# One program per engine for the router and expert stages, with the gather's operands and the last residual reordered

## What is computed

```python
h = rms_norm(x, p["norm2_g"]) * (1.0 + sc2) + sh2
x = x + g2 * moe(h, ...)          # 64 experts, 6 per token, and a shared expert
y = rms_norm(x, final_norm_g)

# moe: top 6 of 64 experts per token, then
a = einsum("td,edf->tef", x, w1)
b = einsum("td,edf->tef", x, w3)
act = silu(a) * b * gates
routed = einsum("tef,efd->td", act, w2)
shared = (silu(x @ ws1) * (x @ ws3)) @ ws2
```

## Time and profile before

| | us |
|---|---|
| three timed runs | 1001.08, 1001.49, 1003.55 (median 1001.49) |
| the profiled execution, whole | 1000.73 |
| its span, first to last instruction | 998.9 |
| PE busy / DVE busy / ACT busy in it | 898.0 / 411.2 / 194.8 |
| DMA over the span | 272.52 MB, mean 273 GB/s |

### The profile page before, as it was taken

How to read it: one execution, slowest core, us unless ns; L and a number is a source line. 1 busy time by engine, 2 the same in 40 slices (tenths; PEclk the granted TensorE clock), 3 DMA queues, 4 the chain that set the end, 5 groups by cost and what they waited for, 6 DMA issues and landing times.

```text
span 998.9 us, 14344 instructions
## 1 busy us (share of the span) xinstructions
PE 898.0 (90%) x5664; PEld 489.4 (49%) x5664; DVE 411.2 (41%) x1006; ACT 194.8 (20%) x422; POOL 99.9 (10%) x100
## 2 busy tenths in 40 slices
PE   2879998999998999979799999899899899899873
PEld 2545767655675554436535345245245245345332
DVE  4695495797021133255323343233223223223137
ACT  4123325100213000150311111211211211211212
POOL 0499970000000000000000000000000000000000
PEclk9678999999997999979899999999999999999996
DMA  9995136120408503012987999999999999999971
GB/s 257 345 368 228 44 127 212 43 85 0 185 20 323 211 1 126 1 63 80 426 345 311 423 425 427 425 426 427 426 426 424 414 425 426 427 425 401 379 320 63
DMA packets 50088, 272.52 MB, mean 273 GB/s; under 512 B 5729, under 2 KB 14343, under 8 KB 21535
## 3 DMA queue, kind: packets, MB, share of 16 engines
q1 hardware_dynamic: 48706, 267.31, 66.1%
q10 hardware_dynamic: 1312, 4.25, 1.4%
HBM read 268.30 MB, written 3.24 MB: 272 GB/s over the span
## 4 chain that ended last, share of the span: by engine, by line
PE 35%; DMA 9%; DVE 3%; SPq 2%; issue 1%; ACT 1%; DVEq 0%
PE bank L1752 15%; PE bank L1789 7%; PE bank L1728 7%; PE bank L1773 5%; DMA sb<-w 4%; DMA sb_W<-w 3%; DMA sb_W<-x_dram 2%; SPq L1129 1%; DVE sb L1911 1%; SPq L1135 0%; ACT sb_Y L1841 0%; DVE sb_W L1978 0%; DVE sb L1977 0%; DVE sb_H L2095 0%; ACT sb L1836 0%
## 5 line engine op out<-in xcount | busy, mean ns | idle before, releaser
L1752 PE MATMUL bank<-sb 128*32 128x512 f32 (+2 forms) x1312 | 188.5, 604 | 12.5 <-DMA sb<-w 6.5
L1752 PEld LDWEIGHTS bank<-sb 128*32 128x32 f32 (+2 forms) x1312 | 56.1, 115 | 110.9 <-issue 110.0
L1728 PE MATMUL bank<-sb_Y,sb_ST 128*128 128x512 f32 x312 | 84.9, 423 | 11.5 <-DVE sb_Y L2013 9.1
L1773 PE MATMUL bank<-sb 128*32 128x512 f32 (+2 forms) x552 | 87.4, 596 | 4.7 <-ACT sb L1836 4.7
L750 PE MATMUL bank<-early 128*128 128x384 f32 x256 | 82.8, 486 | 0.0
L1789 PE MATMUL bank<-sb_S,sb_H 128*128 128x512 f32 (+1 forms) x336 | 75.8, 386 | 6.9 <-ACT sb_H L1868 4.0
L1911 DVE TENSOR_TENSOR sb<-sb,bank 128x512 f32<-128x512 f32 x78 | 53.7, 688 | 62.4 <-PE bank L1728 61.2
L1728 PEld LDWEIGHTS bank<-sb_Y,sb_ST 128*128 128x128 f32 x312 | 56.2, 196 | 45.9 <-issue 20.9
L1789 PEld LDWEIGHTS bank<-sb_S,sb_H 128*128 128x128 f32 x336 | 60.8, 195 | 24.6 <-issue 5.5
L1752 PE MATMUL bank<-sb_W,sb 128*32 128x512 f32 (+1 forms) x160 | 61.2, 635 | 4.9 <-DMA sb<-w 4.9
L750 PEld LDWEIGHTS bank<-early 128*128 128x128 f32 x256 | 48.6, 190 | 33.9 <-issue 0.2
(11 more groups left out here) (289 smaller groups left out, 1104.1 us busy)
## 6 DMA issues: line engine op xcount, KB each, us to landing
sb<-w SPq DMA_DIRECT2D x161, 1024.0 KB, 17.1
sb_W<-w SPq DMA_DIRECT2D x31, 1024.0 KB, 19.5
sb<-w_ada SPq DMA_DIRECT2D x15, 1024.0 KB, 9.1
early<-w_in SPq DMA_DIRECT2D x12, 1024.0 KB, 7.9
early<-w_ada SPq DMA_DIRECT2D x9, 1024.0 KB, 25.5
sb<-w_out SPq DMA_DIRECT2D x1, 4096.0 KB, 17.2
sb<-ada_dram SPq DMA_DIRECT2D x6, 512.0 KB, 15.5
early<-w_proj_s SPq DMA_DIRECT2D x1, 2560.0 KB, 15.4
```

Of the source, the lines that this page charges most:

```text
L1728: ins = nc.tensor.matmul(bank[m % 2][:, :], ST[:, p, j * P:(j + 1) * P], YR[:, x, p % 2, 512 * h:512 * h + 512], start=p == ps[0] and x == ...
L1752: ins = nc.tensor.matmul(bank[2 + p % 2][c0:c0 + w, :], XT[:, c, P * p + c0:P * p + c0 + w], gate_up_weights(units)[:, :, c, :], start=c = ...
L1773: ins = nc.tensor.matmul(bank[y_bank[p][h]][c0:c0 + w, :], hidT[:, f, c0:c0 + w], down_weights(units)[:, f, 512 * h:512 * h + 512], start= ...
```

## The change

The third and fourth block become one block, so that the engines no longer meet between them. Each engine's program of the fourth block follows directly on that of the third. In detail:

- ACT makes Hh between the two SiLUs of the shared expert instead of at the start of the fourth block. DVE fills the gate matrix and makes Hl after cap_full (L1501), ahead of its wait for the positions (PB_DONE), and `block_slots(0)` right after posB and GB.
- New waits: SP waits for the first S (S_ok) and for all products of the shared expert (sy_mm 6) before it loads final_norm_g and the rest of the weights. PE waits for pos_ok ahead of chunk 1 of the first gather and for all eight copies of sy_ok (the shared expert's six and two of the positions) ahead of the first `hidden`. DVE waits for those eight copies ahead of batch 0.
- Memory: sb_W, sb_Y, sb_S, sb_ST, sb_g, sb_fin and sb_H get other places; the residual of the third block (XR), w_s2 and tmpE move too.
- g2b is loaded with a count of its own (g2_in) after `gate_up(6, 3)` and ahead of the last six down weights. The load of X stays behind all weights and waits for units 12 and 13 only.
- DVE in the last batch: ACC times g2b for j = 0 after `add`, for j = 1 and 2 after `down(2)`; X plus ACC for all three after `down(3)`.

```diff
+                sp.wait_ge(S_ok, 1)
+                sp.wait_ge(sy_mm, 2 * NT)
...
                     gate_up(b, 3)
+                    if b == NB - 1:
+                        kind, r = LAST_USER[N_UNITS - 1]
+                        sp.wait_ge(dict(h=h_mm, d=y1_mm)[kind], r + 1)
+                        for r in range(2):
+                            sp.dma_start(g2b[:, r, :], ada_dram[r, 5 * D:6 * D].partition_broadcast(P)).then_inc(g2_in, 16)
                     downward(b, 2)
                     downward(b, 3)
...
-                for u in range(UNITS_SB, N_UNITS):
+                for u in (UNITS_SB, UNITS_SB + 1):
                     kind, r = LAST_USER[u]
                     sp.wait_ge(dict(h=h_mm, d=y1_mm)[kind], r + 1)
-                for r in range(2):
-                    sp.dma_start(g2b[:, r, :], ada_dram[r, 5 * D:6 * D].partition_broadcast(P)).then_inc(fin_in, 16)
                 sp.dma_start(X, x2_dram).then_inc(fin_in, 16)
...
                         if c == 1:
                             wait_last(pe, y_low, rd(2))
+                            if B.first:
+                                pe.wait_ge(pos_ok, 1)
...
                     pe.wait_ge(gates_ok, bt(1, 1))
+                    if B.first:
+                        pe.wait_ge(sy_ok, 2 * NT + 2)
                     hidden(0)
...
                     nc.scalar.activation(hs[:, f], bank[2 + 2 * f][:, 0:TOK], ACT.Silu).then_inc(sh_si, 1)
+                    if f == 0:
+                        act.wait_ge(H_ok, 3)
+                        for j in range(NT):
+                            nc.scalar.activation(Hh[:, j], H[:, j], ACT.Copy).then_inc(h_high_ok, 1)
...
                 ts(cap_full, const[0:E, C_ONE:C_ONE + P], cap_c, float(SB), ALU.mult, ALU.mult).then_inc(sel_ok, 1)
+                ts(k64, iota[:, 0:BATCH], float(SL), float(SL), ALU.mult, ALU.add).then_inc(acc_ok, 1)
+                for x in range(2):
+                    step(ts(gates_id[:, :, x, 0:GC], ...))
+                    nc.vector.tensor_copy(gates_id[:, :, x, GC:GW], ...)
+                for j in range(NT):
+                    dve.wait_ge(h_high_ok, j + 1)
+                    tt(Hl[:, j], H[:, j], Hh[:, j].bitcast(F32), ALU.subtract).then_inc(h_low_ok, 1)
                 dve.wait_ge(pos_mm, PB_DONE)
...
+                block_slots(0)
                 dve.wait_ge(pos_mm, CAP_DONE)
...
-                def before_residual(j):
+                def gated(j):
 
                     if j == 0:
-                        dve.wait_ge(fin_in, 64)
-                    step(tt(ACC[:, j], ACC[:, j], g2b[:, min(j, 1)], ALU.mult))
+                        dve.wait_ge(g2_in, 32)
+                        dve.wait_ge(acc_ok, 12 * NB - 5)
+                    tt(ACC[:, j], ACC[:, j], g2b[:, min(j, 1)], ALU.mult).then_inc(gated_ok, 1)
+
+                def to_residual(j):
+
+                    if j == 0:
+                        dve.wait_ge(fin_in, 32)
+                    dve.wait_ge(gated_ok, j + 1)
                     step(tt(X[:, j], X[:, j], ACC[:, j], ALU.add))
...
                         add(bt, 0)
                         if B.last:
-                            before_residual(0)
+                            gated(0)
                         down(2)
                         if B.last:
-                            before_residual(1)
+                            gated(1)
+                            gated(2)
                         down(3)
                         if B.last:
-                            before_residual(2)
+                            for j in range(NT):
+                                to_residual(j)
...
+                dve.wait_ge(sy_ok, 2 * NT + 2)
                 n = batches(dve, body, overflow_first, overflow_last).per_batch
```

More of the change, by code:

```diff
@@ new lines, in build, with wait_last, __init__, per_batch @@
+        g2_in, gated_ok = sem("g2_in"), sem("gated_ok")
+        NB = len(PLAN)
+        rounds_before = [sum(len(r) for r in ROUNDS[:b]) for b in range(NB)]
+        assert all(len(r) == 4 for r in ROUNDS[1:]) and len(ROUNDS[0]) == 2
+        y_bank = [(5, 6), (5, 6), (5, 6), (2, 1)]
+        def wait_last(eng, s, value):
+            if not isinstance(value, int) or value > 0:
+                eng.wait_ge(s, value)
+        class Static:
+            def __init__(self, b):
+                self.b, self.rounds, self.first, self.last, self.tail = b, ROUNDS[b], b == 0, b == NB - 1, False
+                self.slots = P * len(self.rounds)
+            def per_batch(self, per, off=0):
+                return self.b * per + off
+            def per_round(self, per, off=0):
+                return rounds_before[self.b] * per + off
+            def experts(self, p):
+                return [(c0, w) for c0, w, _ in self.rounds[p]]
+            def weights(self, kind, p):
+                out = []
+                for c0, w, place in self.rounds[p]:
+                    units, _, loaded = UNIT_OF[kind, place]
+                    out.append((c0, w, units, [in_first_stages[u] + n for u, n in zip(units, loaded)]))
+                return out
@@ new lines, in column_tiles, with batches @@
+        def column_tiles(experts):
+            wide = min(w if w != 96 else SB for _, w, *_ in experts)
+            return [(c, wide, *rest) for c0, w, *rest in experts for c in range(c0, c0 + w, wide)]
+        def batches(eng, body, first=None, after=None):
+            for b in range(NB):
+                body(Static(b))
+            eng.wait_ge(tail_ok, 1)
+            more = eng.value_load(ids[0:1, 0:1], min_val=0, max_val=MAXT // BATCH)
+            with eng.If(more > 0):
+                if first:
+                    first()
+                with eng.Fori(0, more) as b:
+                    body(Tail4(b))
+                if after:
+                    after(Tail4(more).tail_batch)
+            return Tail4(more)
@@ L1316, in _ @@
+                scatter(batches(pe, body), -6, 0, (2, 3))
             @block.scalar
@@ L1332, in _ @@
                         act.wait_ge(n2_sq, j)
-                    nc.scalar.activation(at(o_U, D), X[:, j], ACT.Square,
+                    nc.scalar.activation(at(o_U, D), XR[:, j], ACT.Square,
                                          accum_out=nst[:, j:j + 1]).then_inc(n2_sq, 1)
```

623 lines of the change are left out of this document (283 added, 340 removed).

## The result

| | before | after | ratio, 95% interval |
|---|---|---|---|
| first comparison, six runs each | 1001.95 (1000.17 to 1003.55) | 992.0 (988.57 to 992.83) | 0.9892 [0.9872, 0.9913] |
| the same kernel again, later: nine and five runs | 1001.24 (999.62 to 1002.16) | 988.39 (985.11 to 990.02) | 0.9866 [0.9846, 0.9886] |

All times in us. The change makes the kernel faster by 10 to 13 us; the eleven runs of after have their median at 988.9. The forecast was 987.0 with a range of 985.0 to 991.0: the first median lies 1.0 above that range, the second inside it. A second profile of after comes from the later comparison (988.49 us, span 986.7).

The account below looks back on a forecast made before the run. Expert weight loads set the pace from about 550 to 900 us, so PE's first hidden product and DVE's work after X count: 998.9 - 7.9 - 6.1 = 984.9, plus 1.83 is 986.7, forecast 987.0, range 985.0 to 991.0.

Parts of the forecast that it names:

- The front: Shared expert's last product to first hidden product: with the work moved ahead, the hidden product starts 7.9 us sooner.
- the other end (5.8): First gather on PE: if it takes 8.1 us instead of 5.9, the first hidden product gains only 5.8 us.
- The cover on ACT and DVE: Waits in the shared expert: 2.95 us of Hh fit ACT's 12.43, 4.8 us of work fit DVE's 6.42, 1.6 spare.
- That it is carried to the end: Expert weight stream: later loads wait for products, so the dense stretch starts the full 7.9 us sooner, near 541.
- the rival of the slower moved tiles: Loads into moved units 12 to 14: from 0.45 us more per load, over 31 loads, the kernel is slower; 3%.
- The end: After X lands: g2b's products move into DVE's wait, three additions remain, and the residual comes 6.1 us sooner.
- the one on the six down weights: Loads behind g2b: they land 2.5 us later; down(3) delayed by none or 1.4 us, none taken, else gain 4.7.
- the prediction's own sign: At down(3): the forecast is wrong if down(3) waits for a transfer for more than 1.4 us.
- the two counts of 962.4 and 964.1: Last down weight's landing before the change: 962.4 counted forward from the last hidden weights, 964.1 counted back from X.
- The stream swallows the front: Loads between 505 and 549 bound by bytes, not releases: only the end gains, 994.6 us; 6%.
- The end gives nothing: g2b ahead of the six loads holds down(3) back until DVE is as late as before: 992.8 us; 7%.
- It doesn't do what it says: Hl overruns its cover on DVE, PE still stands before the gather, the end is lost: about 1001 us; 3%.

Follow-up runs that it names:

- e5_work_behind: Changed kernel, still one block, with Hh, the gate matrix fill, block_slots(0) and Hl put back behind the shared expert; 996.25 us, ratio 0.9965.
- e9_sums_between: Changed kernel with g2b issued before the last pair of gate and up loads, and DVE's sums with X placed among down(3)'s low parts; 987.87 us.
- e2_end_only: Kernel before with only the new order of g2b's load, the products with it and the sums with X; 996.98 us, ratio 0.9971.
- e8_products_before_down: Changed kernel with 16 transposes of the identity on PE ahead of down(3)'s wait for weights; 989.96 us, ratio 0.9882.
- e3_gates_behind: Changed kernel with g2b's load moved back behind the six down weights, DVE's new order kept; 988.21 us, ratio 0.988.
- e10_products_before_hidden: e9_sums_between plus 20 transposes ahead of the last hidden product's wait for weights, its hid_ok wait moved ahead of both; 985.12 us, ratio 0.9847.

## Why the prediction was right or wrong

**The front: right in size, place and cause.** 7.99 us against 7.9. Gather at a clock of 1.00, as forecast, so the other end (5.8) didn't come. The cover on ACT and DVE held, with 2.10 us left where 1.6 was worked out. In e5_work_behind the same work put behind the shared expert takes all of it back. The rule that the forecast weighed here (the Trainium skill, "TensorE: Matmul & The Clock Gate", "What's actually happening": activity releases the throttle, idling brings it back) agrees: 1.00 without a stand, 0.76 in the stretch with two stands.

**That it is carried to the end: right.** The dense stretch starts at 541 us in the second execution of after, as forecast, and near 545 in the first, which was 2.8 us late already ahead of the gather. 2.3 us of DMA idle are left where 1.2 was forecast. The stretch to the last hidden product but one grew by 0.7 and 1.0 us against the first profile of before. Over all executions with the moved tiles it lies between 438.9 (e5_work_behind) and 442.7 (e9_sums_between), with the old places between 440.5 and 440.8. That speaks against the rival of the slower moved tiles: even 2 us over 31 loads are 0.06 each, and 0.45 was its threshold.

**The end: the mechanism right, one term of the sum mis-sized.** The step that failed is the one on the six down weights: "I take none, being nearer to the row that PE itself shows; the other end is a gain of 4.7." The end gained 4.8 us in the second execution of after and 4.9 in e2_end_only: it was the other end. Also by the prediction's own sign the step was wrong, since `down(3)` waited for a transfer for 2.40 and 1.92 us, more than 1.4. Two sizes were off, and that the other end came out so closely is in part luck. The first is when the last weight landed before: at 963.3, between the two counts of 962.4 and 964.1, so 1.9 us ahead of `down(3)`. The second is the price of g2b ahead of the weights. The sum took 2.5 us, 1 MiB at the rate of the dense stretch; the last weight landed some 3.3 us later (26.6 to 27.0 us behind the last hidden product but one, against 23.4 to 23.6). The trace of before had this price too: there g2b landed at 966.5, 3.1 us behind the last weight. So the count back from X, which also took g2b at 2.5, was 0.8 too late, the delay was 0.8 too short, and their sum, 26.7, was right. The row of PE that I leaned on, `down(3)` waiting for ACT alone, said only that the weight had landed by then, not how long before.

A term that the sum didn't have at all: behind the stand of 2.40 us that this wait makes `down(3)` takes 5.11 us in the first execution, at a mean granted clock of 0.71. That is 1.5 us more, and the end there gained 3.0. I priced the wait and not what PE's clock may do behind it, though the front's argument had just been made of that. Why the clock was low there and not behind the stands of 1.92 and 1.97 us in the second execution and in e2_end_only stays open; one execution shows it.

The first execution against the forecast of its span, 984.9, term by term from the table (the second in brackets): stages ahead of the change +3.2 (+0.3), to the shared product -0.4 (-0.3), the front -0.1 (-0.1), the rounds +0.7 (+1.0), the end +3.1 (+1.3), behind it -0.4 (-0.3). Together +6.1 (+1.8), which are 991.0 and 986.7. The forecast of 987.0 had moreover taken only part of the offset of the median: 986.7 and 0.76 are 987.5.

**The range: the scatter was mis-sized.** I gave the runs' own scatter as 0.4 us. The runs shown spread by 2.5, those of the second table line by 4.9, fourteen runs of before from 998.51 to 1003.98. The term of +3.2 is a piece of it: nothing that the change touches runs there. Windows of 10 us out of that stretch, first after, then after's second execution, then before:

```profile
163.00:173.00 10.00, 9.16 (x84) 7.32 (x84) 0.75 (x2) 3.96 (x12) 0.00 (x0) 0.52 0.91 288
```

```profile
163.00:173.00 10.00, 9.31 (x137) 7.47 (x138) 0.51 (x2) 5.94 (x18) 0.00 (x0) 0.83 0.84 266
```

```profile
163.00:173.00 10.00, 9.58 (x139) 7.85 (x140) 0.25 (x2) 6.13 (x20) 0.00 (x0) 0.83 0.86 273
```

The same code, behind a stand of 2.79, 3.19 and 2.72 us: 84 products in one execution and 137 or 139 in the others, at a granted clock of 0.52 and 0.83. The twelve other profiled executions of this work reach L750 at 178.2 to 180.4 us. With a scatter of 4 us in the range the first median would have lain in it. Whether the other high runs of the first comparison (992.0 to 992.5) were high for the same reason isn't known: only one of the six has a profile. The second median, 988.39, lies below the 988.9 that the range's upper end makes without its 2.1 for a slow gather, which didn't come; the first lies above all of it.

**The rivals.** The stream swallows the front: no (990.38 with the front alone). The end gives nothing: no, but its mechanism, g2b ahead of the six weights, is the one that took 1.3 of the 6.1 us, and 3.1 with the low clock behind the wait. It doesn't do what it says: no. Slower by the moved tiles: no.

Open: whether the order with the sums between is faster on the clock than the change. Its trace is, by 3.7 us behind the last hidden product against the second execution of after, but with g2b in the gap that product starts 8.5 to 10.3 us behind the one before it (four executions), where it was 7.6 to 7.9; that gives 0.6 us or more of it back, and 987.87 against 988.39 can't be told apart with these runs.

## What to carry to other kernels

A load that is pulled forward for one engine stands in front of others on the same queue: find when the last of those lands in the trace of before, and price the load by what that same load took there (3.1 us for g2b) and not by the rate of the dense stretch (2.5). A wait that ends on something else says nothing of how much slack there was. Price a new stand of PE twice, once for the wait and once, as the range's other end, for the product behind it at the lower clock. And where a kernel's PE stands often, its single executions differ by more than their medians suggest: look at the spread of the runs that are there before setting the ends of a range.

## What the runs showed of the hardware that was not expected

How long PE stood, here between 2.8 and 3.7 us, doesn't tell at which clock it goes on. The last hidden product, 64 products of one shape, takes 7.07 us behind its wait for weights, or 8.3 to 8.8. Its waits and durations in different executions: 2.77 us and 7.07 (after), 2.89 and 7.07 (e8_products_before_down), 2.87 and 8.77 (e3_gates_behind), 2.89 and 8.77 (e5_work_behind), 3.31 and 8.35 (e10_products_before_hidden), 3.69 and 7.07 (e9_sums_between). Nor does the drop come with the stand's end. In the second execution of before, PE at 872 us:

```profile
872.37 0.63 PE L1752 MATMUL bank<-sb 128*32 128x512 f32 x3 [3.00 <-DMA sb_W<-w]
...
873.32 1.14 PE L1752 MATMUL bank<-sb 128*32 128x512 f32 x3
...
876.64 0.63 PE L1752 MATMUL bank<-sb 128*32 128x512 f32 x3
```

The first products behind the stand run at the full rate, those from 873 to 876 us take 1.14 instead of 0.63, and then the full rate is back: the engine was at work again when the clock fell (granted clock 0.96 up to 873.2, 0.51 from there to 876.6, 1.00 behind it; 0.51 is the level of 1.2 GHz). The Trainium skill, "TensorE: Matmul & The Clock Gate", "What's actually happening", says that one kernel shows different numbers of slow products from run to run. That agrees with the two executions of after, whose `down(3)` takes 5.11 and 3.64 us. For a change of 1% it matters: it made 1.5 us at `down(3)` and some 3 ahead of L750 in one execution.
